# A mixed attention block on one Trainium2 core: the first slab of x and the first weight strip in halves, the first products taken product by product, the squares in other steps

## The reference, cut to what matters

```python
u = x * rsqrt(mean(x * x, axis=-1) + 1e-6) * norm_gain        # 512 x 2048
proj = u @ w_in                                                # 2048 -> 13392 columns
(q_sb, k_sb, v_sb, z_sb, q_sa, k_sa, v_sa, z_sa,
 q_ix, k_ix, w_ix, g_sb, g_sa) = split(proj)
y_sb = (stick_breaking_attention(q_sb, k_sb, v_sb) * silu(z_sb)) @ w_branch_sb
y_sa = (attention over 128 indexed keys(q_sa, k_sa, v_sa, q_ix, k_ix, w_ix) * silu(z_sa)) @ w_branch_sa
h = x + (sigmoid(g_sb) * y_sb + sigmoid(g_sa) * y_sa) @ w_out
out = h * rsqrt(mean(h * h, axis=-1) + 1e-6) * final_norm_gain
```

## Time and profile before

| what | value |
|---|---|
| median of 3 executions | 1597.68 us (1597.47 to 1597.71) |
| profiled execution, its own time | 1597.08 us |
| its span, first to last instruction | 1595.5 us |
| PE busy | 1585.0 us, 99% of the span |
| DVE busy | 821.9 us, 52% |
| ACT busy | 572.5 us, 36% |
| mean granted TensorE clock | 0.999 |

### The profile page before, as it was taken

How to read it: one execution, slowest core, us unless ns; L and a number is a source line. 1 busy time by engine, 2 the same in 40 slices (tenths; PEclk the granted TensorE clock), 3 DMA queues, 4 the chain that set the end, 5 groups by cost and what they waited for, 6 DMA issues and landing times.

```text
span 1595.5 us, 19959 instructions
## 1 busy us (share of the span) xinstructions
PE 1585.0 (99%) x7138; PEld 1317.2 (83%) x7138; DVE 821.9 (52%) x1183; ACT 572.5 (36%) x851; POOL 15.8 (1%) x35
## 2 busy tenths in 40 slices
PE   9999999999999999999999999999999999999997
PEld 7788888888888888888888888888888888888886
DVE  6853678522126655556564546554545545434333
ACT  5542333222224444334453332343332533323232
POOL 0000000000000000000000000000000000000000
PEclk9999999999999999999999999999999999999999
DMA  7223323333333333333334334333433522253223
GB/s 225 82 79 93 93 80 93 106 92 85 100 105 96 111 108 110 111 106 104 106 117 132 109 102 113 98 116 110 115 91 122 181 101 92 96 204 121 98 100 118
DMA packets 97979, 176.39 MB, mean 111 GB/s; under 512 B 11264, under 2 KB 24080, under 8 KB 97296
## 3 DMA queue, kind: packets, MB, share of 16 engines
q1 hardware_dynamic: 93712, 160.60, 33.4%
q0 software_dynamic: 3040, 13.63, 2.3%
q10 hardware_dynamic: 1184, 1.58, 0.3%
HBM read 156.90 MB, written 8.39 MB: 104 GB/s over the span
## 4 chain that ended last, share of the span: by engine, by line
PE 97%; ACT 1%; DVE 1%; DMA 1%; issue 0%; SPq 0%; ACTq 0%; DVEq 0%
PE proj L1178 29%; PE proj L1179 29%; PE proj L1180 29%; PE attn L1179 3%; PE attn L1180 3%; PE attn L1178 3%; DMA xs<-in_x 1%; PE attn L1313 1%; PE attn L1312 1%; ACT junk L463 0%; ACT w_hi L410 0%; DVE w_lo L721 0%; DVE xs L764 0%; DVE area L764 0%; ACT u_hi L443 0%
## 5 line engine op out<-in xcount | busy, mean ns | idle before, releaser
L1178 PE MATMUL proj<-u_hi,w_hi 128*128 128x512 f32 x1536 | 600.5, 391 | 0.5 <-DVE u_lo L774 0.5
L1180 PE MATMUL proj<-u_hi,w_lo 128*128 128x512 f32 x1536 | 598.9, 390 | 0.0
L1179 PE MATMUL proj<-u_lo,w_hi 128*128 128x512 f32 x1536 | 598.8, 390 | 0.0
L721 DVE TENSOR_TENSOR w_lo<-stage,w_hi 128x1024 fp32r<-128x1024 f32 x266 | 323.5, 1222 | 458.7 <-ACT w_hi L410 457.2
L410 ACT ACTIVATE w_hi<-stage 128x1024 fp32r<-128x1024 f32 x266 | 280.1, 1056 | 430.9 <-PE proj L1180 302.2
L1178 PEld LDWEIGHTS proj<-u_hi,w_hi 128*128 128x128 f32 x1536 | 288.8, 188 | 60.2 <-issue 1.3
L1180 PEld LDWEIGHTS proj<-u_hi,w_lo 128*128 128x128 f32 x1536 | 288.5, 188 | 60.2
L1179 PEld LDWEIGHTS proj<-u_lo,w_hi 128*128 128x128 f32 x1536 | 288.8, 188 | 58.7
L1178 PE MATMUL proj<-w_hi,u_hi 128*128 128x512 f32 x256 | 99.9, 390 | 0.0
L1180 PE MATMUL proj<-w_hi,u_lo 128*128 128x512 f32 x256 | 99.8, 390 | 0.0
L1179 PE MATMUL proj<-w_lo,u_hi 128*128 128x512 f32 x256 | 99.8, 390 | 0.0
(11 more groups left out here) (175 smaller groups left out, 1413.0 us busy)
## 6 DMA issues: line engine op xcount, KB each, us to landing
stage<-in_w_in SPq DMA_DIRECT2D x208, 512.0 KB, 3.7
stage<-in_w_out SPq DMA_DIRECT2D x32, 512.0 KB, 3.6
x_in<-turned SPq DMA_DIRECT2D x256, 40.0 KB, 1.9
stage<-in_w_branch_sb SPq DMA_DIRECT2D x16, 512.0 KB, 3.6
stage<-in_w_branch_sa SPq DMA_DIRECT2D x16, 512.0 KB, 4.1
xs<-in_x SPq DMA_DIRECT2D x8, 512.0 KB, 8.0
o_scratch<-og POOLq DMA_DIRECT2D x16, 256.0 KB, 2.3
hres<-in_x POOLq DMA_DIRECT2D x1, 4096.0 KB, 13.6
```

What stands on the lines that cost most here:

```text
L721: V.tensor_tensor(w_lo[:, s % RING, :, :], stage[:, s % 2, :, :], w_hi[:, s % RING, :, :].bitcast(F), ALU.subtract).then_inc(strip_lo, 1)
L1178: nc.tensor.matmul(out_, a_hi, b_hi, start=start, stop=False, skip_group_check=free)
L1179: nc.tensor.matmul(out_, a_hi, b_lo, start=False, stop=False, skip_group_check=free)
L1180: return nc.tensor.matmul(out_, a_lo, b_hi, start=False, stop=stop, skip_group_check=free)
```

## The change

Slab 0 of x and strip 0 of the weight are each loaded as two halves of 128 columns and of one tile of 128 rows, in the order x half 0, strip half 0, x half 1, strip half 1, with semaphores of their own for the first halves. After that SyncE's order is slab 1, strip 1, slab 2, strip 2, slabs 3 and 4, strip 3, slabs 5 to 7. The high part of strip half 0 is made by DVE (a copy, ahead of everything else on DVE) instead of ACT; DVE makes its low part next, then the low part of tile 0, then the low part of strip half 1, then that of tile 1. On ACT the high part of strip half 1 now stands ahead of `turned_high(1)`. PE turns tile 0, runs three blanks instead of four, and takes the first strip product by product: the four `w_hi*u_hi` of tile 0, then `turn_x(1)`, then the four `w_hi*u_lo`, the four `w_lo*u_hi`; tile 1 in the same order after the turns of tiles 2 and 3. The eight squares stand in the steps as 2, 3 and 3 (steps 0, 1, 2), and none ahead of the loop.

```diff
--- before.py
+++ after.py
@@ -217,6 +217,7 @@
     gain_loaded, ixw_loaded, consts, masks = sem("gain_loaded"), sem("ixw_loaded"), sem("consts"), sem("masks")
     sumsq, norm_step, rooted = sem("sumsq"), sem("norm_step"), sem("rooted")
     cols_ready, cols_turned, row_ready = sem("cols_ready"), sem("cols_turned"), sem("row_ready")
+    x_first, first_loaded = sem("x_first"), sem("first_loaded")
     first_hi, first_lo = sem("first_hi"), sem("first_lo")
     raw_ready, raw_scaled, un_hi_ready, un_lo_ready = (
         sem("raw_ready"), sem("raw_scaled"), sem("un_hi_ready"), sem("un_lo_ready"))
@@ -307,16 +308,18 @@
             def first_strip(s):
                 load_strip(C_QIX, s, rows(win)(s)[:, :, COL_QIX:COL_QIX + CW])
 
-            load_x(0)
-            first_strip(0)
+            for k, x_sem, w_sem in ((0, x_first, first_loaded), (1, x_loaded[0], strip_loaded[0])):
+                sp.dma_start(xs[:, :, P * k:P * k + P], x_cols[:, :, P * k:P * k + P]).then_inc(x_sem, 16)
+                sp.dma_start(stage[:, 0, k, :], rows(win)(0)[:, k, COL_QIX:COL_QIX + CW]).then_inc(w_sem, 16)
             load_x(1)
             first_strip(1)
-            for p in range(2, 5):
-                load_x(p)
+            load_x(2)
             first_strip(2)
+            load_x(3)
+            load_x(4)
+            first_strip(3)
             for p in range(5, NS):
                 load_x(p)
-            first_strip(3)
             sp.dma_start(ixw[:, :, :], win[:, :, COL_KIX:COL_KIX + KW]).then_inc(ixw_loaded, 16)
             for s in range(4, NS):
                 first_strip(s)
@@ -470,23 +473,21 @@
             act.wait_ge(gain_ready, 1)
             turned_high(0)
             act.wait_ge(strip_loaded[0], 16)
-            A(w_hi[:, 0, 0, :], stage[:, 0, 0, :], ACT.Copy).then_inc(first_hi, 1)
+            A(w_hi[:, 0, 1, :], stage[:, 0, 1, :], ACT.Copy).then_inc(strip_hi, 1)
             turned_high(1)
-            A(w_hi[:, 0, 1, :], stage[:, 0, 1, :], ACT.Copy).then_inc(strip_hi, 1)
             split_hi(0, 1)
             turned_high(2)
             turned_high(3)
-            for i in range(QT):
-                sum_of_squares(i, 0)
+
+            SQUARES_AT = ((0, 1), (2, 3, 4), (5, 6, 7)) + ((),) * (NS - 3)
 
             def in_first(s):
                 def f():
                     if s + 2 < NS:
                         turned_pair(s + 2)
-                    if s in (1, 2):
-                        for i in (2 * s - 2, 2 * s - 1):
-                            sum_of_squares(i, 1)
-                    elif s == 3:
+                    for n in SQUARES_AT[s]:
+                        sum_of_squares(n % QT, n // QT)
+                    if s == 3:
                         act.wait_ge(norm_step, 2)
                         A(root[:, :], var[:, :], ACT.Sqrt).then_inc(rooted, 1)
                         act.wait_ge(ixw_loaded, 16)
@@ -785,15 +786,17 @@
                     V.tensor_tensor(by_tile(u_lo[:, k, :]), raw_u(k), by_tile(u_hi[:, k, :].bitcast(F)),
                                     ALU.subtract).then_inc(un_lo_ready, 1)
 
-            dve.wait_ge(gain_ready, 1)
-            turned_low(0)
+            dve.wait_ge(first_loaded, 16)
+            V.tensor_copy(w_hi[:, 0, 0, :], stage[:, 0, 0, :]).then_inc(first_hi, 1)
             dve.wait_ge(first_hi, 1)
             V.tensor_tensor(w_lo[:, 0, 0, :], stage[:, 0, 0, :], w_hi[:, 0, 0, :].bitcast(F),
                             ALU.subtract).then_inc(first_lo, 1)
-            turned_low(1)
+            dve.wait_ge(gain_ready, 1)
+            turned_low(0)
             dve.wait_ge(strip_hi, 1)
             V.tensor_tensor(w_lo[:, 0, 1, :], stage[:, 0, 1, :], w_hi[:, 0, 1, :].bitcast(F),
                             ALU.subtract).then_inc(strip_lo, 1)
+            turned_low(1)
             turned_raw(0)
             turned_raw(1)
             split_lo(0, 1)
@@ -1219,7 +1222,9 @@
                         steps[s]()
 
             def turn_x(k):
-                if k % 2 == 0:
+                if k == 0:
+                    pe.wait_ge(x_first, 16)
+                elif k == 1 or k % 2 == 0:
                     pe.wait_ge(x_loaded[k // 2], 16)
                 if k >= HEAD_START:
                     pe.wait_ge(raw_ready, bank_user(k) + 1)
@@ -1246,23 +1251,29 @@
             nc.tensor.transpose(kw_bank[:, 0:KT], gain_rows[0:KT, :], ident[0:KT, 0:KT]).then_inc(gain_turned, 1)
             keep_busy(1)
             turn_x(0)
-            turn_x(1)
-            keep_busy(4)
+            keep_busy(3)
 
             def first_strip():
 
                 for j in range(2):
-                    pe.wait_ge(u_lo_ready, j + 1)
-                    if j == 0:
-                        pe.wait_ge(first_lo, 1)
-                    else:
+                    def products(w, u, first=False):
+                        for e in range(4):
+                            m = nc.tensor.matmul(proj[e][:, :], w[:, 0, j, P * e:P * e + P], u[:, j, :],
+                                                 start=first, stop=False)
+                        return m
+
+                    if j:
                         turn_x(2)
                         turn_x(3)
-                        pe.wait_ge(strip_lo, 1)
-                    for e in range(4):
-                        cols = slice(P * e, P * e + P)
-                        m = mm3(proj[e][:, :], w_hi[:, 0, j, cols], w_lo[:, 0, j, cols],
-                                u_hi[:, j, :], u_lo[:, j, :], j == 0, False)
+                    pe.wait_ge(u_hi_ready, j + 1)
+                    pe.wait_ge(strip_hi if j else first_hi, 1)
+                    products(w_hi, u_hi, first=j == 0)
+                    if j == 0:
+                        turn_x(1)
+                    pe.wait_ge(u_lo_ready, j + 1)
+                    products(w_hi, u_lo)
+                    pe.wait_ge(strip_lo if j else first_lo, 1)
+                    m = products(w_lo, u_hi)
                 m.then_inc(strip_used, 1)
 
             def between_strips(s):
```

## The result

The changed kernel takes 1600.14 us, the median of 22 runs (1598.29 to 1601.59); the kernel before takes 1597.68 in its 22 runs beside it (1597.10 to 1598.79). The ratio is 1.0015 (95% interval 1.0009 to 1.0022): 2.5 us slower, less than the 0.2% named in the prediction, but clear of noise. The spread has grown from 1.7 to 3.3 us. The profiled execution took 1600.56, with a span of 1598.9: 3.48 us more than the profiled one of before.

A forecast was written before the change was run, and what follows sets the result against it. The ACT and DVE chain sets PE's last wait; eight squares add 4.6 us, 3.1 paid by the earlier loop start, so 1597.68 + 1.46 = 1599.1 us. Own range 1598.7 to 1599.6; 8 in 10: 1597.8 to 1601.2.

The forecast's parts named there:

- What bounds it: Ahead of 45 us, an ACT and DVE chain sets PE's last wait; a step with three squares loses 1.24 us against PE.
- The clock: PE's clock around the roughly 3 us pause before the columns' turn: cost between 0 and 2.3 us, taken as 0.
- clock falls in the hole: Rival: clock falls in PE's pause before the columns' turn, adding 0.5 to 2.3 us; 1599.6 to 1601.4, chance 0.13.
- the named case: The forecast itself: PE passes its last wait, at the columns' turn, 1.46 us later, 1599.1 us; chance 0.56.
- three signs: Wrong if strip 5's high part starts before 35, the pause before the columns' turn is short, or products behind stand 0.43 apart.
- The sum of the chain: ACT and DVE steps up to strip 5's high part at 36.2, 1.46 us late, putting the columns' turn at 43.7.
- the loads: Loads in halves and SyncE's new order, at the start: strip 2 issued at 8.0, landed at 13.9; priced at nothing.
- tile 1's high part: On ACT in the first strip: starts at 9.2 instead of 7.34, behind a turn ending at 8.95.
- The start: PE's first real product at about 6.6 instead of 8.35; PE itself gains 0.55 us in the first strip.
- the clock rises with the first products: Rival: PE's clock is high from 6.6, tile 1's high part ends one us sooner; +0.4 us, 1598.1, chance 0.11.
- The other side: Rival: squares on ACT don't bind, strip 5's high part starts by 34.73; at best 1.6 us sooner, 1596.1; chance 0.05.
- within 0.2%: Whole kernel's time stays within 3.2 us of no change; chance 0.93.

The follow-up runs named there:

- e1: Kernel before with one edit: the eight squares stand in steps 0, 1, 2 as 2, 3, 3, none ahead of the loop; 1600.69 us, +3.49.
- e4: Changed kernel with one square of each step placed inside ACT's wait for DVE's raw copies; 1595.96 us, -1.24 to the kernel before.
- e2: Changed kernel with twelve blank matmuls in PE's pause ahead of the norm columns' turn; 1598.63 us, +1.43 to the kernel before.
- e9: The changed kernel run again, unaltered, in a later group; 1599.81 us, +2.52 to the kernel before.
- e8: Changed kernel with six blank matmuls ahead of the wait for the norm's columns; 1598.78 us, +1.47 to the kernel before.
- e7: Changed kernel with squares and order of loads behind the first strip as in the kernel before; 1597.89 us, +0.58 to the kernel before.
- e11: Second run of e4 with strip 4's load moved ahead of the indexer's narrow weight; 1595.00 us, -2.29 to the kernel before.
- e5: Kernel before with squares 0, 1 ahead of the loop, 2, 4, 6 inside ACT's wait for raw copies, 3, 5, 7 outside; 1596.42 us, -0.78.
- e12: e5 run again in a later group; 1596.28 us, -1.01 to the kernel before.
- e3: Changed kernel with slab 0 and strip 0 loaded whole, as before; 1599.43 us, +2.12 to the kernel before.

## Why the prediction was right, and where it was off

**What bounds it: right, and shown.** The last wait of PE ahead of 45 us ends a chain on ACT and DVE, and three squares in a step put it behind PE. Marks forecast at 21.0, 28.6, 36.2, columns' turn 43.7; measured 21.55, 29.23, 36.82, 44.32. e1 shows the squares alone doing it, e4 shows it undone by their places alone.

**The clock: the term that failed.** The step says "The bounds are 0 and 2.3; I take 0", from a pause of 0.5 us, far from the 3.1 that it forecast. The profiled execution lost 1.39 there, and by e2 it is 1.0 in the median, which is what the forecast lacks (2.46 - 1.46). So what happened is the rival that had 0.13, clock falls in the hole, middle 1600.5, and not the named case with its 0.56, whose own range (1.0 to 1.9 us slower) the measured 2.46 misses. Of the three signs by which the prediction called itself wrong, one came: products behind the pause stand 0.43 apart. The number still lies in the wider range because that range was drawn to hold half of the falling clock. The rule of the Trainium skill (TensorE: Matmul & The Clock Gate, Part 1) that the clock returns to half rate after the array has been idle for long was what spoke against this change, and the traces of the changed kernel, e1 and e9 agree: clock 0.50 behind pauses of 3.3 to 3.4 us.

**The sum of the chain: right in its total, in part by luck.** Where the fall is kept away, e2 and e8 cost 1.43 and 1.47, and the sum had 1.46. The columns' turn, forecast at 43.7, came at 44.32, and at 43.95, 43.80 and 44.20 in e9, e2 and e8. But on the way two steps were wrong, in opposite directions. One is the loads: "I price all of this at nothing". Half 1 of strip 0 was forecast at 6.75 and landed at 7.70; strip 2's load, forecast to be issued at 8.0 and to land by 13.9, was issued at 9.10 and landed at 15.09, and DVE's raw copies of tile 4 came at 17.35 instead of 16.8. I took "the same bytes lie ahead of it" for the same landing. Strip 1's load, issued at 3.48 behind the two more issues instead of 2.50, put its high part at 10.68 instead of 9.9. In e9 it is this load, and not strip 2's, that starts the chain (pieces of the chain that ended last):

```profile
3.48 7.46 DMA stage<-in_w_in
10.94 0.02 issue
10.96 1.07 ACT w_hi L413
12.03 0.02 issue
12.06 1.23 DVE w_lo L722
```

From 12.06 on DVE runs there without a pause, as forecast, and reaches the raw copies at 16.97. The other step is tile 1's high part: forecast at 9.2 behind a turn at the low clock, it came at 8.26, as the clock had risen early. The one took back what the other gave.

**The start: the clock rises with the first products,** the rival of 0.11, is what this execution shows: 0.23 from 6.49 on. It brought PE 1.6 us instead of the forecast 0.55 by 13.33, but the forecast of +0.4 for that case didn't follow, since the chain hung on the loads and not on tile 1's turn. PE lost 0.86 of it again at 34.38, where the prediction says that strip 4 isn't held, and stood for 3.38 in front of the columns, near the 3.1 of the forecast. Nor is the early rise a property of the new start: in e7 and e11, with the same head, the first four products take 1.69 and 1.51 us instead of 0.93, so most of them still stand 0.43 apart, nearly as forecast. The timeline of PE in e7:

```profile
6.60 1.85 PE L1263 MATMUL proj<-u_hi,w_hi 128*128 128x512 f32 x4
8.29 0.60 PE L1234 MATMUL attn<-ident,xs 128*128 128x128 f32 x4
```

**The other side** (the squares don't bind) is excluded by e1. The share of "within 0.2%" held: +2.46 of 3.2.

## What to carry to other kernels

Work on a helper engine that seems idle most of the time is free only inside a wait of that engine; look for its loop's own period, step by step, and compare it with the period of the engine that bounds. Moving the same eight squares cost 3.5 us in one set of places and won 0.8 and 1.0 in another (e5 and e12), without one instruction more. An earlier start of the busy engine is worth nothing while another chain sets its last wait, and it even makes PE's pauses ahead of that wait longer (1.48 us at strip 2 in e7, 0.53 in the kernel before). A pause of about 3 us cost the clock on top in many runs here, though no run shows that the earlier start alone brings it about. Take the chain out first, then measure the start.

## What the runs showed of the hardware

The clock can fall after the pause is over. In e1 the columns' turn starts at 44.69 after 3.30 us of pause, four products stand at the high distance, and from 46.16 on they are 0.43 apart, for eight products. Windows of e1:

```profile
45.00:46.00 1.00, 1.00 (x8) 0.87 (x6) 1.00 (x2) 0.00 (x0) 0.00 (x0) 1.00 0.00 0
46.00:47.00 1.00, 1.00 (x4) 0.73 (x3) 1.00 (x2) 0.00 (x0) 0.00 (x0) 0.52 0.00 0
47.00:48.00 1.00, 1.00 (x4) 0.80 (x3) 1.00 (x3) 0.14 (x1) 0.00 (x0) 0.50 0.00 0
```

What one such pause costs differs from run to run of one kernel: five products in the changed kernel, eleven or twelve in e9, which are 1.39 and some 2.7 us. All three profiled executions with a pause of 3.3 us or more lost the clock; the one with 2.85 (e3) and the one with 1.96 (e8) didn't. Both kernels have single runs 1.7 us above their medians or more. For e3 the mean granted clock of these runs tells more: it is 0.997 in its four slowest (1600.69 to 1601.16) and 0.998 or 0.999 in the other seven. 0.997 stands as well for 14 of the 22 runs of the changed kernel and for four of 11 in e1 and in e9, and for no run of any other kernel here, among them 99 of the kernel before. So the pause of e3 costs the clock in some runs too. For the two slow runs of e8, at 0.998 like most of its others, it stays open.

The time at which the clock first rises differs as well, by the distances: about 8.9 in the kernel before and 9.9 in e5, which has the same start; ahead of 6.49 in the changed kernel and near 8 in e7 and e11, which have its start.

With the first loads split, the rate was lower: from 4 to 8 us the queues moved 280 GB/s in the changed kernel, against 338 in the kernel before and 363 in e3. It is 250 to 294 in all eight profiled executions with halves and 338 to 376 in all six with whole loads. Half 1 of the strip landed 1.0 us later than the whole strip did before. The halves bring rows of 512 bytes instead of 1024 for slab 0, and two more issues; which of the two costs the rate was not separated.
